# Attention's softmax jobs by twos, with bias and mask added on TensorE, in a two-block model on one NeuronCore

## The chip, the cores and the metric

One core of a Trainium2 chip runs the whole program. The metric is the device time of one execution in microseconds (us). The engines are named as the profile names them: PE (TensorE matmul; PEld is its weight load), DVE (VectorE), ACT (ScalarE), POOL (GpSimd), SP (SyncE, which issues DMAs). PE's results land in PSUM, which has 8 banks of 512 float32 per partition.

## What is computed

The program is a chain of two models of two layers each, over 512 positions of width 1024: first a mixer and a mixture-of-experts layer, twice, and then attention and a gated feed-forward layer, twice. Only the attention of the second model is touched. It has three kinds of heads, four of each, all computed by query blocks of 128:

```
def chunk_mask(qi, ki):
    return (ki[None, :] // CHUNK_2) <= (qi[:, None] // CHUNK_2)          # CHUNK_2 = 64
...
        sc = jnp.einsum('bhqd,bhkd->bhqk', qb, k).astype(jnp.float32) * scale
        p = jax.nn.softmax(sc + bias_fn(qi, ki), axis=-1).astype(v.dtype)
        return jnp.einsum('bhqk,bhkd->bhqd', p, v)
# fox:  bias = where(ki <= qi, cum[q] - cum[k], NEG), width 64, scale 64 ** -0.5
# diff: bias = where(chunk_mask, -slope[h] * abs(q - k), NEG), two softmaxes (q1 k1, q2 k2) of width 64 over one v of width 128
# mla:  bias = where(chunk_mask, 0, NEG), width 96, scale 96 ** -0.5, v of width 64
    x = x + jnp.concatenate([o_fox, o_diff, o_mla], axis=-1) @ w_o[i]
```

All is float32.

## The kernel before, in words

Each engine has its instruction list written out by hand; semaphores hand data over. `Handoff` is a kind of PSUM bank with a `full` and a `free` count; `Banks.take` goes round all 8 banks and makes PE wait until the last owner of a bank has freed it.

Attention of a layer is made of **jobs**: one head (or one of diff's two softmaxes) and one query block. Block qc sees n = 128 (qc + 1) keys, and the blocks go in the order 3, 1, 2, 0 (n = 512, 256, 384, 128). There are 16 mla jobs, 32 diff jobs and 16 fox jobs in each of the two layers. A job has three parts, and `pipeline` goes through them with a lag: at step m every engine does `turn` of job m - 3, `scores` of job m, `values` of job m - 4.

- `tensor_scores`: PE multiplies q (K rows by 128) with k (K rows by n) into a bank, as a plain float32 matmul, which the profile shows as two matmuls (two passes). K is 96 for mla and 64 for diff and fox: diff's two softmaxes lie on rows 0 to 63 and 64 to 127, and so do fox's even and odd heads. For fox two bf16 matmuls more add the bias (6 rows, L1915) and the causal mask of the last 128 columns (L1916).
- `vector_scores`: for mla and diff, DVE reads the bank, scales, adds the bias or mask (L2137, into SBUF tile PB) and takes the maximum (L2138). For fox it only takes the maximum from the bank (L2122). For each diff head DVE first makes that head's bias tile BT (L2128).
- `scalar_scores`: ACT takes the exponential with the row sum (L2029), from PB for mla and diff, from the bank for fox.
- `tensor_turn`, `scalar_turn`: PE transposes each 128 by 128 piece into a bank (L1931), and ACT copies it to SBUF (L2037).
- `tensor_values`, `vector_values`: PE multiplies with v (L1939), two passes for each 128 keys, and DVE scales by the reciprocal of the sum.

Between these parts lie products of the layer with its weights, on PE lines L600 and L602: v of diff (`dv`) after some diff steps, fox's q and k (`fqk`), fox's v (`fv`, 96 matmuls of 256 columns), and the output product, whose first half is followed by `rest_of_third`, the end of fox's jobs. During fox's steps 5 to 10 one transposed feature of the output (L508) is made at a step.

## Time and profile before

| | |
|---|---|
| time, median of 3 runs | 2738.56 us (2738.56 to 2741.27) |
| profiled execution, its own time | 2739.48 us |
| its span in the profile | 2738.1 us |
| PE busy | 2631.8 us (96%) |
| DVE, ACT, POOL busy | 1205.6, 909.4, 360.0 us |
| attention's jobs and products, layer 0 | about 1470 to 1670 us of the span |
| the same, layer 1 | about 2143 to 2345 us of the span |

In the rows below, a row of the timeline is one run of like instructions: its start, the time from its first start to its last end, engine, line, operation, tiles, shapes, count, and in brackets idle time before it. Matmuls overlap in their records (each has a latency), so what one costs is read from the distance between the starts of neighbouring rows. PEclk is the clock that TensorE was granted, 1.00 being full.

### The profile page before, as it was taken

To read this page: it belongs to the slowest core of one execution; us is meant where nothing else is said; L and a number is where in the kernel's file an instruction comes from. 1 tells how busy PE (TensorE), PEld (TensorE's weight loads), DVE (VectorE), ACT (ScalarE), POOL (GpSimd) and SP (SyncE) were. 2 spreads that over 40 slices of the span, in tenths; PEclk is the share of its full clock that TensorE was granted. 3 is DMA by queue.
4 is the path that set the end of the run, shared out by engine and by line. 5 is a ranking of instruction groups with operands and counts; after the bars stand their busy time and mean duration, and the time that the engine had idled before them with its cause. 6 is when DMAs were issued, how large, how long until landed. Compare 5 with 4: busy or idle time off the path is not lost.

```text
span 2738.1 us, 33170 instructions
## 1 busy us (share of the span) xinstructions
PE 2631.8 (96%) x13288; PEld 1828.3 (67%) x13288; DVE 1205.6 (44%) x2337; ACT 909.4 (33%) x1740; POOL 360.0 (13%) x167
## 2 busy tenths in 40 slices
PE   7989999999878999999989999999999999999999
PEld 6865444444756544445467678888888767888887
DVE  2543233232746223223357643562554664355264
ACT  4431111111473111111254453442345445443233
POOL 3200000000331000000020011222222101122122
PEclk9999999999998999999999999999999999999999
DMA  5229999999313999999822011223132101223212
GB/s 203 72 98 420 419 421 421 421 421 384 108 47 133 417 421 421 421 421 421 353 73 78 32 62 49 95 94 116 62 112 84 58 16 62 78 93 108 77 62 85
DMA packets 139004, 543.42 MB, mean 198 GB/s; under 512 B 18784, under 2 KB 30304, under 8 KB 89696
## 3 DMA queue, kind: packets, MB, share of 16 engines
q1 hardware_dynamic: 129232, 536.94, 50.2%
q10 hardware_dynamic: 9616, 4.32, 0.6%
q8 instruction: 108, 1.77, 0.3%
q14 instruction: 48, 0.39, 0.0%
HBM read 539.12 MB, written 2.10 MB: 198 GB/s over the span
## 4 chain that ended last, share of the span: by engine, by line
PE 93%; DVE 3%; ACT 2%; issue 1%; DMA 1%; POOL 0%; SPq 0%; DVEq 0%; ACTq 0%
PE ps L600 24%; PE ps L1362 16%; PE ps L602 15%; PE ps L1384 8%; PE ps L1337 5%; PE ps L622 4%; PE ps L534 3%; PE ps L1939 3%; PE ps L1397 3%; PE ps L1919 2%; PE ps L1398 2%; PE ps L1931 1%; PE ps L535 1%; PE ps L1914 1%; PE ps L452 1%
## 5 line engine op out<-in xcount | busy, mean ns | idle before, releaser
L600 PE MATMUL ps<-w,w 128*128 128x512 f32 x2976 | 681.5, 391 | 2.6 <-POOL w L277 2.6
L600 PEld LDWEIGHTS ps<-w,w 128*128 128x128 f32 x2976 | 560.3, 189 | 120.0 <-POOL w L277 3.4
L277 POOL TENSOR_TENSOR w<-w,w 128x1024 fp32r<-128x1024 f32 (+2 forms) x139 | 336.3, 2429 | 2219.0 <-ACT w L269 2219.0
L1362 PE MATMUL ps<-w,w 128*64 128x512 f32 x2048 | 451.6, 594 | 1.8 <-issue 1.8
L602 PE MATMUL ps<-w,w 128*128 128x512 f32 (+1 forms) x1872 | 416.4, 385 | 18.3 <-issue 15.2
L602 PEld LDWEIGHTS ps<-w,w 128*128 128x128 f32 x1872 | 345.0, 193 | 85.9 <-issue 19.8
L269 ACT ACTIVATE w<-w 128x1024 fp32r<-128x1024 f32 (+2 forms) x260 | 252.9, 1000 | 438.0 <-PE ps L600 197.4
L277 DVE TENSOR_TENSOR w<-w,w 128x1024 fp32r<-128x1024 f32 (+2 forms) x121 | 195.5, 1623 | 386.3 <-ACT w L269 383.9
L1362 PEld LDWEIGHTS ps<-w,w 128*64 128x64 f32 x2048 | 146.0, 137 | 285.6 <-issue 285.6
L1614 DVE TENSOR_TENSOR X<-ps,X 128x512 f32<-128x512 f32 x256 | 163.1, 683 | 163.2 <-PE ps L1398 162.2
L1384 PE MATMUL ps<-w,w 128*64 128x512 f32 x1024 | 226.8, 595 | 0.8 <-ACT w L1448 0.8
L2363 DVE SCALAR_TENSOR_TENSOR w<-ps,PK,w 128x511 f32<-128x511 f32 (+1 forms) x176 | 131.9, 749 | 75.5 <-ACT w L2319 72.4
L1384 PEld LDWEIGHTS ps<-w,w 128*64 128x64 f32 x1024 | 70.6, 137 | 139.8 <-issue 138.9
L1337 PE MATMUL ps<-w,w 128*128 128x256 f32 x1024 | 131.0, 287 | 4.9 <-DVE w L1585 4.9
L1337 PEld LDWEIGHTS ps<-w,w 128*128 128x128 f32 x1024 | 130.0, 196 | 7.6 <-DVE w L1585 5.1
L1602 DVE TENSOR_TENSOR w<-ps,w 128x512 f32<-128x512 f32 x32 | 34.8, 1086 | 212.0 <-PE ps L1362 212.0
L622 PE MATMUL ps<-w,w 128*128 128x512 f32 x528 | 122.0, 390 | 0.0
L1397 PE MATMUL ps<-w,w 128*128 128x512 f32 x256 | 111.8, 437 | 4.6 <-DVE w L1621 4.6
L1621 DVE SCALAR_TENSOR_TENSOR w<-ps,w,w 128x512 fp32r<-128x512 f32 x64 | 45.1, 747 | 159.0 <-ACT w L1493 159.0
L622 PEld LDWEIGHTS ps<-w,w 128*128 128x128 f32 x528 | 98.8, 188 | 20.3
L1493 ACT ACTIVATE w<-ps,w 128x512 fp32r<-128x512 f32 x64 | 40.6, 684 | 204.0 <-PE ps L1384 204.0
L534 PE MATMUL ps<-w,w 128*128 128x256 f32 x768 | 98.7, 292 | 9.7 <-POOL w L277 6.5
(256 smaller groups left out, 2471.0 us busy)
## 6 DMA issues: line engine op xcount, KB each, us to landing
w<-in_moe_w_gate SPq DMA_DIRECT2D x128, 1024.0 KB, 14.5
w<-in_moe_w_up SPq DMA_DIRECT2D x128, 1024.0 KB, 16.8
w<-in_moe_w_down SPq DMA_DIRECT2D x128, 1024.0 KB, 13.6
w<-in_w_up SPq DMA_DIRECT2D x40, 1024.0 KB, 5.1
w<-in_w_down SPq DMA_DIRECT2D x20, 1024.0 KB, 5.1
w<-in_w_in SPq DMA_DIRECT2D x16, 1024.0 KB, 5.1
w<-in_ab_w_in SPq DMA_DIRECT2D x10, 1024.0 KB, 5.2
w<-in_c_w_in SPq DMA_DIRECT2D x8, 1024.0 KB, 5.1
```

Of the source, the lines that this page charges most:

```text
L269: up(self.whi, self.S.e.activation(hi, raw, ACT.Copy))
L277: up(self.wlo[self.low[s][0]], lane.e.tensor_tensor(lo, raw, hi.bitcast(F32), ALU.subtract))
L534: return pe.matmul(bs[o][:, t], w[:, P * o:P * o + P], a(k)[:, t], start=first, stop=stop)
L600: ins = pe.matmul(bank[:, :], wp[:, k, P * o:P * o + P], ap(k0 + k), start=first, stop=stop)
L602: ins = pe.matmul(bank[:, 0:width], ap(k0 + k)[:, P * o:P * o + P], wp[:, k, :], start=first, stop=stop)
L622: ins = pe.matmul(bank_of(o)[:, 0:width], ap(k)[:, P * o:P * o + P], wp, start=(k == 0 and pi == 0), stop=(hi is rows[-1][0] and pi == 2))
L1337: i = pe.matmul(bank[:, 256 * k:256 * k + 256], HB[part][:, c, t:t + P], SELR[:, c, :], start=(part == 0 and c == 0), stop=(part == 1 and ...
L1362: ins = pe.matmul(bank[64 * e:64 * e + 64, :], XG[p % 3][:, 4 * u + k, 64 * e:64 * e + 64], w[e][:, k, :], start=(u == 0 and k == 0), stop ...
L1384: ins = pe.matmul(two[n][64 * e:64 * e + 64, :], HDT[:, 2 * u + k, 64 * e:64 * e + 64], w[e][:, k, 512 * n:512 * n + 512], start=(u == 0 a ...
L1397: pe.matmul(bank[:, :], s_, YH[:, 512 * n:512 * n + 512], start=True, stop=False)
L1614: up(bx.free, dve.tensor_tensor(x, bank[:, :], x, ALU.add))
L2363: ins = dve.scalar_tensor_tensor(y[:, d:T], bank[:, 0:T - d], col("conv_w_2", 132 * i + 44 * tap + f), y[:, d:T], ALU.mult, ALU.add)
```

## The change

Jobs are taken by twos. At step p each engine does `turn` of pair p - 2, `scores` of pair p, `values` of pair p - 3. A pair is two jobs of one list that follow each other: diff's two softmaxes of one head and block, fox's heads 0 and 1 (or 2 and 3) at one block, mla's blocks 3 and 1 (or 2 and 0) of one head. Both score matmuls of a pair are issued first, then the bias matmuls, then the masks: a far bias of diff for the columns ahead of the last 128 (3 rows, bf16), and for the last 128 columns a bf16 matmul of the identity with a constant tile that holds mask and near bias. The scales move into the copies of q. DVE's addition and its bias tiles are gone, ACT reads all scores from PSUM, and one reciprocal serves two jobs. Scores always take banks 0 to 3; everything else within attention's pipeline takes banks 4 to 7. The constants shrink from 1971 to 1715 words a row, and POOL's two casts at the start go.

```diff
-LAG = 3
 TAIL = 4
+ALL_BANKS, SCORE_BANKS, OTHER_BANKS = tuple(range(8)), (0, 1, 2, 3), (4, 5, 6, 7)
 BLOCKS = (3, 1, 2, 0)
...
+    ("identb", 64), ("causalb", 64), ("blockb", 64), ("nearb", 256), ("far_q", 256), ("far_k", 192),
...
-    def take(self, kind):
-        self.i = (self.i + 1) % 8
-        while self.t[self.i] in self.held:
-            self.i = (self.i + 1) % 8
-        if self.owner[self.i]:
-            before, k = self.owner[self.i]
+        self.PE, self.among, self.last = PE, ALL_BANKS, {ALL_BANKS: 7}
+    def take(self, kind, among=None):
+        among = among or self.among
+        i = self.last[among] = among[(among.index(self.last.get(among, among[-1])) + 1) % len(among)]
+        if self.owner[i]:
+            before, k = self.owner[i]
             self.PE.wait_total(before.free, k)
-        kind.banks.append(self.t[self.i])
-        self.owner[self.i] = (kind, len(kind.banks))
-        return self.t[self.i]
+        kind.banks.append(self.t[i])
+        self.owner[i] = (kind, len(kind.banks))
+        return self.t[i]
...
+                    for two in range(2) for qc in BLOCKS for h in (2 * two, 2 * two + 1)]
...
             scores, turn, values = engine
-            nj = len(jobs)
-            for m in steps:
-                if m in at_step:
-                    at_step[m]()
-                if LAG <= m < nj + LAG:
-                    turn(m0 + m - LAG, jobs[m - LAG])
-                if m < nj:
-                    scores(m0 + m, jobs[m])
-                if m > LAG:
-                    values(m0 + m - LAG - 1, jobs[m - LAG - 1])
+            for p in steps:
+                if p in at_step:
+                    at_step[p]()
+                for lag, part in ((2, turn), (0, scores), (3, values)):
+                    m = 2 * (p - lag)
+                    if 0 <= m < len(jobs):
+                        part(m0 + m, jobs[m:m + 2])
         def two_kinds(engine, dv, fqk):
-            n = len(mla_jobs) + len(diff_jobs)
-            pipeline(mla_jobs + diff_jobs, 0, engine, {M_DIFF + LAG: dv, n: fqk}, range(n + LAG + 1))
+            n = M_FOX // 2
+            pipeline(mla_jobs + diff_jobs, 0, engine, {M_DIFF // 2 + 2: dv, n: fqk}, range(n + 4))
         def third_kind(engine, fv, o_feature):
-            at_step = {LAG: fv}
-            for n, k in enumerate(FEATURES_OUT[:6]):
-                at_step[LAG + 2 + n] = lambda k=k: o_feature((k,))
-            pipeline(fox_jobs, M_FOX, engine, at_step, range(len(fox_jobs)))
+            at_step = {2: fv}
+            for n in range(3):
+                at_step[4 + n] = lambda n=n: o_feature(FEATURES_OUT[2 * n:2 * n + 2])
+            pipeline(fox_jobs, M_FOX, engine, at_step, range(len(fox_jobs) // 2))
...
-        def tensor_scores(m, job):
-            qc, kind, h, q, k, _, _ = job
-            n = P * (qc + 1)
-            if kind == "fox":
-                bank = banks.take(bfs)
-                of_head = slice(32 * h, 32 * h + 6)
+            n = len(fox_jobs) // 2
+            pipeline(fox_jobs, M_FOX, engine, {}, range(n, n + 4))
+        def tensor_scores(m, two):
+            taken = [banks.take(bsc, SCORE_BANKS) for _ in two]
+            for bank, (qc, _, _, q, k, _, _) in zip(taken, two):
+                n = P * (qc + 1)
                 pe.matmul(bank[:, 0:n], q, k[:, 0:n], start=True, stop=False)
-                pe.matmul(bank[:, 0:n], turned_q[of_head, P * qc:P * qc + P], turned_k[of_head, 0:n], start=False, stop=False)
-                up(bfs.full, pe.matmul(bank[:, n - P:n], CTB[:, 0, :], CTB[:, 1, :], start=False, stop=True))
-            else:
-                bank = banks.take(bsc)
-                up(bsc.full, pe.matmul(bank[:, 0:n], q, k[:, 0:n], start=True, stop=True))
-        def wait_exp(lane, m, job):
-            if job[1] == "fox":
-                lane.wait_ge(bfs.free, m - M_FOX + 1)
-            else:
-                lane.wait_ge(ex, m + 1)
-        def tensor_turn(m, job):
-            wait_exp(PE, m, job)
-            bank = banks.take(bpt)
-            for j in range(job[0] + 1):
-                ins = pe.transpose(bank[:, P * j:P * j + P], PB[m % (LAG + 1)][:, P * j:P * j + P], ident)
-            up(bpt.full, ins)
-        def tensor_values(m, job):
-            qc, vals, dv = job[0], job[5], job[6]
-            PE.wait_ge(bpt.free, m + 1)
-            bank = banks.take(bo)
-            for j in range(qc + 1):
-                ins = pe.matmul(bank[:, 0:dv], PTB[m % 2][:, P * j:P * j + P], vals(j), start=(j == 0), stop=(j == qc))
-            up(bo.full, ins)
+            for bank, (qc, kind, h, _, _, _, _) in zip(taken, two):
+                n = P * (qc + 1)
+                if kind == "fox":
+                    rows_ = slice(32 * h, 32 * h + 6)
+                    pe.matmul(bank[:, 0:n], turned_q[rows_, P * qc:P * qc + P], turned_k[rows_, 0:n], start=False, stop=False)
+                elif kind != "mla" and qc:
+                    rows_ = slice(64 * int(kind[-1]), 64 * int(kind[-1]) + 3)
+                    pe.matmul(bank[:, 0:n - P], far_q[rows_, P * h:P * h + P], far_k[rows_, T - n:T - P], start=False, stop=False)
+            for bank, (qc, kind, h, _, _, _, _) in zip(taken, two):
+                n = P * (qc + 1)
+                near = {"mla": cst_bf16("blockb"), "fox": cst_bf16("causalb")}.get(kind, near_diff[:, P * h:P * h + P])
+                up(bsc.full, pe.matmul(bank[:, n - P:n], cst_bf16("identb"), near, start=False, stop=True))
+        def tensor_turn(m, two):
+            for m, job in zip((m, m + 1), two):
+                PE.wait_ge(bsc.free, m + 1)
+                bank = banks.take(bpt)
+                for j in range(job[0] + 1):
+                    ins = pe.transpose(bank[:, P * j:P * j + P], PB[m % 4][:, P * j:P * j + P], ident)
+                up(bpt.full, ins)
+        def tensor_values(m, two):
+            for m, (qc, _, _, _, _, vals, dv) in zip((m, m + 1), two):
+                PE.wait_ge(bpt.free, m + 1)
+                bank = banks.take(bo)
+                for j in range(qc + 1):
+                    ins = pe.matmul(bank[:, 0:dv], PTB[m % 4][:, P * j:P * j + P], vals(j), start=(j == 0), stop=(j == qc))
+                up(bo.full, ins)
...
+            banks.among = OTHER_BANKS
             two_kinds(engine, values_of_diff, queries_of_fox)
...
-                    banks.held = bx.banks[-NT:]
+                    banks.among = OTHER_BANKS
                     rest_of_third(engine)
                     PE.wait_ge(bo.free, M_FOX + len(fox_jobs))
                     tensor_o_features(FEATURES_OUT[6:])
-                    banks.held = ()
+                    banks.among = ALL_BANKS
...
+            banks.among = SCORE_BANKS
...
-        def scalar_scores(m, job):
-            qc, kind, h = job[0], job[1], job[2]
-            n = P * (qc + 1)
-            p = PB[m % (LAG + 1)]
-            scores = p
-            if kind == "fox":
-                scores = bfs.next(S)
-                S.wait_ge(bpt.full, m - LAG)
-            S.wait_ge(mx, m + 1)
-            up(bfs.free if kind == "fox" else ex,
-               act.activation(p[:, 0:n], scores[:, 0:n], ACT.Exp, bias=AT[:, m % 8:m % 8 + 1],
-                              accum_out=AT[:, 8 + m % 8:9 + m % 8]))
-        def scalar_turn(m, job):
-            n = P * (job[0] + 1)
-            bank = bpt.next(S)
-            if m > 1:
-                S.wait_ge(bo.full, m - 1)
-            up(bpt.free, act.activation(PTB[m % 2][:, 0:n], bank[:, 0:n], ACT.Copy))
-        def scalar_values(m, job):
+        def scalar_scores(m, two):
+            for m, job in zip((m, m + 1), two):
+                n = P * (job[0] + 1)
+                bank = bsc.next(S)
+                if m > 3:
+                    S.wait_ge(bpt.full, m - 3)
+                S.wait_ge(mx, m + 1)
+                up(bsc.free, act.activation(PB[m % 4][:, 0:n], bank[:, 0:n], ACT.Exp, bias=AT[:, m % 8:m % 8 + 1],
+                                            accum_out=AT[:, 8 + m % 8:9 + m % 8]))
+        def scalar_turn(m, two):
+            for m, job in zip((m, m + 1), two):
+                n = P * (job[0] + 1)
+                bank = bpt.next(S)
+                if m > 3:
+                    S.wait_ge(bo.full, m - 3)
+                up(bpt.free, act.activation(PTB[m % 4][:, 0:n], bank[:, 0:n], ACT.Copy))
...
-            scalar_product(("dq", i), scalar_banks(lambda m: DQ[:, m, :]))
+            scalar_product(("dq", i), scalar_banks(lambda m: DQ[:, m, :], scale=0.125))
...
-                    bank_to(T_[0:96, h, :], bank[0:96, :])
+                    bank_to(T_[0:96, h, :], bank[0:96, :], scale=96 ** -0.5 if T_ is QT else 1.0)
...
-        def vector_scores(m, job):
-            qc, kind, h = job[0], job[1], job[2]
-            n = P * (qc + 1)
-            if kind == "fox":
-                bank = bfs.next(V)
+        def vector_scores(m, two):
+            for m, job in zip((m, m + 1), two):
+                n = P * (job[0] + 1)
+                bank = bsc.next(V)
                 up(mx, dve.tensor_reduce(AT[:, m % 8:m % 8 + 1], bank[:, 0:n], AX, ALU.max, negate=True))
-                return
-            scale = 96 ** -0.5 if kind == "mla" else 0.125
-            if kind == "diff0" and qc == BLOCKS[0]:
-                if h > 1:
-                    V.wait_ge(bsc.free, m - 8)
-                vstep(dve.scalar_tensor_tensor(BT[:, h % 2, :], cst("dist"), -slopes[h], mask, ALU.mult, ALU.add))
-            if kind == "mla":
-                bias = mask[:, 512 - n:512]
-            else:
-                bias = BT[:, h % 2, 512 - n:512]
-            p = PB[m % (LAG + 1)][:, 0:n]
-            bank = bsc.next(V)
-            if m > LAG:
-                V.wait_ge(bpt.full, m - LAG)
-            V.wait_total(bsc.free, up(bsc.free, dve.scalar_tensor_tensor(p, bank[:, 0:n], scale, bias, ALU.mult, ALU.add)))
-            up(mx, dve.tensor_reduce(AT[:, m % 8:m % 8 + 1], p, AX, ALU.max, negate=True))
-        def vector_turn(m, job):
-            wait_exp(V, m, job)
-            sm = AT[:, 8 + m % 8:9 + m % 8]
+        def vector_turn(m, two):
+            V.wait_ge(bsc.free, m + 2)
+            sm = AT[:, 8 + m % 8:10 + m % 8]
             up(rc, dve.reciprocal(sm, sm))
...
-                    up(bv.free, dve.tensor_copy(T_[0:96, h, :], bank[0:96, :]))
+                    up(bv.free, dve.tensor_scalar(T_[0:96, h, :], bank[0:96, :], 96 ** -0.5 if T_ is QT else 1.0, None, ALU.mult))
...
-            up(ctb, pool.tensor_copy(CTB[:, j, :], cst(name)))
```

PE's instruction order in diff's jobs, layer 0, before: the end of a step, two jobs of block 3 (128x512 scores of w_20480 and w_22528, which are DQ and DK; w_16384 is v, w_14336 the copied transposes). `order` counts a float32 matmul once.

```order
L1931 MATMUL ps<-CT,w_12288_11029 128x128 [waits s_scores_free,s_exp]
L1931 MATMUL ps<-CT,w_12288_11029 128x128 x2
L1919 MATMUL ps<-w_22528_11038,w_20480_11036 128x512 [waits s_values_free]
L1939 MATMUL ps<-w_16384_11039,w_14336_11030 128x128 [waits s_turned_free]
L1939 MATMUL ps<-w_16384_11039,w_14336_11030 128x128 x2
L1931 MATMUL ps<-CT,w_12288_11029 128x128 [waits s_scores_free,s_exp]
L1919 MATMUL ps<-w_22528_11038,w_20480_11036 128x512 [waits s_values_free]
L1939 MATMUL ps<-w_16384_11039,w_14336_11030 128x128 [waits s_turned_free]
L1939 MATMUL ps<-w_16384_11039,w_14336_11030 128x128 x2
```

The same place now (L1912 scores, L1920 far bias, L1924 near bias and mask):

```order
L1931 MATMUL ps<-CT,w_12288_11027 128x128 [waits s_turned_free,s_scores_free]
L1931 MATMUL ps<-CT,w_12288_11027 128x128 x2
L1931 MATMUL ps<-CT,w_12288_11027 128x128 [waits s_turned_free,s_scores_free]
L1931 MATMUL ps<-CT,w_12288_11027 128x128 x2
L1912 MATMUL ps<-w_22528_11035,w_20480_11033 128x512 x2
L1920 MATMUL ps<-CT 128x384 x2
L1924 MATMUL ps<-CT 128x128 x2
L1939 MATMUL ps<-w_16384_11036,w_14336_11028 128x128 [waits s_values_free]
L1939 MATMUL ps<-w_16384_11036,w_14336_11028 128x128
L1939 MATMUL ps<-w_16384_11036,w_14336_11028 128x128 [waits s_values_free]
L1939 MATMUL ps<-w_16384_11036,w_14336_11028 128x128
```

The two score matmuls now stand next to each other, with two transposes' groups before them and two values' groups behind, and each turn waits for the copy (s_turned_free) of the pair before, in the same two banks.

PE's order in fox's jobs, layer 0, before (junk holds the bias's parts, CTB the identity and the mask):

```order
L1931 MATMUL ps<-CT,w_12288_11029 128x128 [waits s_values_free]
L1931 MATMUL ps<-CT,w_12288_11029 128x128
L1914 MATMUL ps<-w_20480_11042 128x512 [waits s_bank_feat_free]
L1915 MATMUL ps<-junk 128x512
L1916 MATMUL ps<-CTB 128x128
L1939 MATMUL ps<-w_22528_11043,w_14336_11030 128x64 [waits s_turned_free]
L1939 MATMUL ps<-w_22528_11043,w_14336_11030 128x64 x3
```

And a fox step now:

```order
L1931 MATMUL ps<-CT,w_12288_11027 128x128 [waits s_values_free,s_scores_free] x2
L1912 MATMUL ps<-w_20480_11039 128x256 x2
L1917 MATMUL ps<-junk 128x256 x2
L1924 MATMUL ps<-CT 128x128 x2
L1939 MATMUL ps<-w_22528_11040,w_14336_11028 128x64 [waits s_bank_feat_free]
L1939 MATMUL ps<-w_22528_11040,w_14336_11028 128x64 x2
L1939 MATMUL ps<-w_22528_11040,w_14336_11028 128x64 [waits s_bank_feat_free]
L1939 MATMUL ps<-w_22528_11040,w_14336_11028 128x64 x2
```

The same three forms of matmul are there for each job, now in twos of each form; the values' banks are now freed by the features (s_bank_feat_free) made in the same step.

## Rows read from the trace of the kernel before

**Rows 1.** The page: PE's busy time; the chain that ended last, by engine.

```profile
PE 2631.8 (96%) x13288; PEld 1828.3 (67%) x13288; DVE 1205.6 (44%) x2337; ACT 909.4 (33%) x1740; POOL 360.0 (13%) x167
...
PE 93%; DVE 3%; ACT 2%; issue 1%; DMA 1%; POOL 0%; SPq 0%; DVEq 0%; ACTq 0%
```

**Rows 2.** Windows: stretch, length, busy PE, PEld, DVE, ACT, POOL, PEclk, DMA.

```profile
1476.58:1493.30 16.72, 16.72 (x114) 13.12 (x114) 14.89 (x49) 11.64 (x39) 0.00 (x0) 1.00 0.01 1
1529.50:1571.40 41.90, 41.90 (x228) 27.44 (x227) 35.20 (x111) 23.31 (x72) 0.00 (x0) 1.00 0.00 1
1615.00:1642.00 27.00, 27.00 (x169) 17.66 (x166) 13.69 (x43) 15.23 (x44) 2.42 (x1) 1.00 0.25 79
```

**Rows 3.** Timeline of PE, diff's jobs, layer 0.

```profile
1529.58 1.12 PE L1919 MATMUL ps<-w,w 64*128 64x512 f32 x2
...
1542.27 0.48 PE L1919 MATMUL ps<-w,w 64*128 64x128 f32 x2
1542.69 0.71 PE L1939 MATMUL ps<-w,w 128*128 128x128 f32 x4
1543.23 0.49 PE L1931 MATMUL ps<-CT,w 128*128 128x128 f32 x3
1543.65 1.12 PE L1919 MATMUL ps<-w,w 64*128 64x512 f32 x2
1544.71 0.94 PE L1939 MATMUL ps<-w,w 128*128 128x128 f32 x6
```

**Rows 4.** Timeline of PE, the bf16 transposes ahead of mla's jobs, and mla's jobs, layer 0.

```profile
1469.81 0.61 PE L1983 MATMUL ps<-CTB,w 128*128 128x128 bf16 x8
...
1481.13 1.02 PE L1919 MATMUL ps<-w,w 96*128 96x512 f32 x2
1482.07 1.10 PE L1939 MATMUL ps<-w,w 128*128 128x64 f32 x8
...
1486.65 1.02 PE L1919 MATMUL ps<-w,w 96*128 96x512 f32 x2
```

**Rows 5.** Timeline of PE, fox's jobs, layer 0.

```profile
1632.79 0.60 PE L1931 MATMUL ps<-CT,w 128*128 128x128 f32 x4
...
1634.50 1.12 PE L1914 MATMUL ps<-w 64*128 64x512 f32 x2
1635.56 0.39 PE L1915 MATMUL ps<-junk 6*128 6x512 bf16 x1
1635.88 0.23 PE L1916 MATMUL ps<-CTB 128*128 128x128 bf16 x1
1635.94 1.06 PE L1939 MATMUL ps<-w,w 128*128 128x64 f32 x8
...
1640.66 0.61 PE L1931 MATMUL ps<-CT,w 128*128 128x128 f32 x4
```

**Rows 6.** The chain, experts' matmuls on column halves (64 of 128 columns).

```profile
218.60 13.97 PE ps L1362 x64
```

**Rows 7.** Timeline of PE: first turn of mla, values behind fqk.

```profile
1474.37 0.66 PE L1931 MATMUL ps<-CT,w 128*128 128x128 f32 x4 [1.35 <-ACT w L2029]
...
1595.36 0.94 PE L1939 MATMUL ps<-w,w 128*128 128x128 f32 x6 [0.91 <-ACT w L2037]
```

**Rows 8.** Windows: the fv product of layer 0 and of layer 1.

```profile
1600.87:1614.11 13.24, 13.24 (x98) 13.03 (x97) 9.37 (x23) 11.37 (x34) 2.59 (x1) 0.87 0.06 25
...
2274.79:2288.99 14.20, 14.20 (x98) 13.99 (x97) 10.86 (x24) 10.96 (x31) 2.52 (x1) 0.80 0.04 15
```

**Rows 9.** Lines by form, fox's jobs: count, busy us, mean ns.

```profile
L2037 ACT ACTIVATE w<-ps 128x512 f32<-128x512 f32 x4 | 2.4, 590 | 0.0
...
L2029 ACT ACTIVATE w<-ps,AT 128x512 f32<-128x512 f32 x3 | 2.1, 688 | 4.3 <-DVE AT L2122 4.3
L2122 DVE TENSOR_REDUCE AT<-ps 128x1 f32<-128x512 f32 x3 | 2.1, 684 | 2.8 <-PE ps L1916 2.8
```

**Rows 10.** The chain, its first piece.

```profile
2.74 13.75 DMA w<-in_ab_w_in
```

More of the change, by code:

```diff
@@ L1852, in attention @@
         turned_q, turned_k = junk[:, 0:T], junk[:, T:2 * T]
-        mask = cst("mask")
+        near_diff, far_q, far_k = (cst_bf16(name) for name in ("nearb", "far_q", "far_k"))
         lam_init = 0.8 - 0.6 * math.exp(-0.3 * i)
-        slopes = [2.0 ** (-2.0 * (h + 1)) for h in range(4)]
         up_unit = W.of[("up", i)][0]
@@ new lines, in vector_turn, with vector_values @@
+        def vector_turn(m, two):
+            V.wait_ge(bsc.free, m + 2)
+            sm = AT[:, 8 + m % 8:10 + m % 8]
+            up(rc, dve.reciprocal(sm, sm))
+        def vector_values(m, two):
+            for m, (qc, kind, h, _, _, _, dv) in zip((m, m + 1), two):
+                sm = AT[:, 8 + m % 8:9 + m % 8]
+                bank = bo.next(V)
+                V.wait_ge(rc, m // 2 + 1)
+                if kind == "diff0":
+                    up(bo.free, dve.tensor_scalar(O1B[:, qc, :], bank[:, 0:dv], sm, None, ALU.mult))
+                elif kind == "diff1":
+                    V.wait_ge(nlam, 1)
+                    V.wait_ge(bo.free, m)
+                    vstep(dve.tensor_tensor(sm, sm, LS[:, 3:4], ALU.mult))
+                    o = O[:, qc, 256 + P * h:384 + P * h]
+                    up(bo.free, dve.scalar_tensor_tensor(o, bank[:, 0:dv], sm, O1B[:, qc, :], ALU.mult, ALU.add))
+                else:
+                    c0 = (768 if kind == "mla" else 0) + 64 * h
+                    up(bo.free, dve.tensor_scalar(O[:, qc, c0:c0 + 64], bank[:, 0:dv], sm, None, ALU.mult))
```

74 lines of the change are left out of this document (31 added, 43 removed).

## The prediction

> **What bounds it now.** I read the page first: PE is busy 2631.8 of 2738.1 us and 93% of the chain is PE [rows 1]. So only PE time, or a wait of PE, is worth anything. Then the windows of the three kinds of jobs: PE is busy through all of 16.72, 41.90 and 27.00 us, while DVE has 14.89, 35.20 and 13.69 and ACT 11.64, 23.31 and 15.23 [rows 2]. The addition that DVE loses is therefore cover, not path; what counts is PE's instruction list, and whether the others still keep ahead of it.
>
> Then the timeline, by distances between starts. A score matmul of a 64-row job takes 0.42 us for 128 columns and 1.06 for 512 [rows 3]. The difference, 0.64, is three times 128 columns in two passes: **0.107 us for a pass of 128 columns**. A head has 4 + 2 + 3 + 1 = 10 such pieces. An mla head (96 rows) takes 1486.65 - 1481.13 = 5.52 [rows 4]: less 20 pieces in passes (2.13) that leaves 3.39 for 10 transposes and 20 passes of values, **0.113 each**, and nothing over. A diff head has 8 jobs in 1543.65 - 1529.58 = 14.07 [rows 3]: 60 x 0.113 = 6.78 and 40 x 0.107 = 4.27 leave 3.02, so **0.38 us a job is lost to the 64-row form**. It shows where PE changes form: 0.42 - 0.21 = 0.21 in the scores, 0.42 - 3 x 0.11 = 0.09 between transposes and scores, 0.54 - 4 x 0.113 = 0.09 at the first values. I split it into entering the form (0.20: drain and a weight load that shows) and leaving it (0.20). A fox head takes 1640.66 - 1632.79 = 7.87 [rows 5]: 3.39 + 2.13, bias 0.53 (512 columns in 0.32, of which 0.11 is a change of form, so 0.053 for 128), four masks of 0.06, and 1.58 over, 0.39 a job.
>
> The Trainium skill (TensorEngine Tiling, Key Properties) says that changing the tiling mode drains TensorE; the trace agrees, with 0.38 for a 64-row job and none for a 96-row one.
>
> **The change, part by part.** (1) *Diff.* A pair enters the 64-row form once (0.20), leaves through the 3-row form and back (0.20), not twice each. Its passes are issued A1 A2 B1 B2. A1 and A2 share rows and follow each other, B2 follows B1; only A2 and B1 can run at once, so I count three passes for four. That two tiles of the array do run at once is shown only for column halves: 64 matmuls of 512 columns in 13.97 us are 0.218 each [rows 6], half of a pass of 512 (0.427). I carry that over to row halves, with 0.04 for the late start of the second (between nothing and a weight load, 0.11). Far bias, bf16 on rows 0 and 64: 0.053 for 128 columns, also side by side, + 0.04. Two near masks 0.12. A head then has 3 x 10 x 0.107 = 3.20, far bias 6 x 0.053 = 0.32, three pairs with fixed 0.20 + 0.04 + 0.20 + 0.04 + 0.12 = 0.60, and one without far bias 0.46, so 2.26, and 6.78 as before: 12.56 against 14.07, -1.5; eight heads **-12.0**.
>
> (2) *Fox*, two heads: 3.20 + 0.53 + 4 x 0.60 + 6.78 = 12.91 against 2 x 7.87 = 15.74, -2.8; four such twos **-11.3**.
>
> (3) *Mla* gets a mask matmul for each job and no overlap (96 rows). The eight bf16 transposes take 0.61 [rows 4], about 0.06 each in a stream; 32 x 0.06 = **+1.9** (bounds 0 and 0.113 each: 0 to +3.6).
>
> (4) *Waits.* At mla's start PE waits 1.35 us for the first exponential [rows 7], after three jobs' scores. Now four jobs' scores go first (2.5 us of work), and the first exponential needs scores of 1.45, a maximum of 0.69 and an exponential of 0.69 [rows 9] with some 0.4 of handing over: 3.3, a wait of about 0.8. With the smaller wait for the first copy gone: -0.7 a layer, **-1.4**. Behind fqk the values wait 0.91 for ACT's copy [rows 7], since ACT first empties four banks and splits a weight; a longer list (pair's turn and another pair's values) covers part: -0.4 a layer, **-0.8**. Bounds for both: 0 and -5.
>
> (5) *Nothing:* DVE's addition, the bias tiles, half of the reciprocals, exponentials from PSUM (688 ns for 512, fox already does it [rows 9]): all beside PE. If DVE's cover were gone, it would have shown in mla, where DVE is at 14.89 of 16.72. *Constants:* 256 words less on 128 rows is 0.13 MB ahead of the first weights, whose landing begins the chain [rows 10]: **-0.3**. *Banks:* scores' four are asked for again two steps on, when their exponentials are needed anyway. Turned and values now have two banks each. The tight chain is ACT's: after a block 3 pair's scores come a maximum of 0.69, two exponentials of 0.79 with their sums, two copies of block 1 or 2 (0.4 to 0.5) and handovers, 3.3 to 3.5 us, before the next turn but one may take its banks; PE has 0.9 of values and a step of 2.9 to do meanwhile. It fits by 0.3 to 0.5. Products take the same four banks one each 0.7 us, so the last values are emptied in time. 0, bounds 0 and +6.
>
> Sum: -12.0 - 11.3 + 1.9 - 1.4 - 0.8 - 0.3 = **-23.9**. From 2739.5, the profiled execution's own time, that is 2715.6; the median of the runs is 0.9 lower, so **2715 us**.
>
> By the Trainium skill (TensorE: Matmul & The Clock Gate, Part 3) four row tiles gave 3.07 times, not 4; an estimate from that is 1.3 passes for two at once, 0.3 x 10 x 0.107 x 12 = +4, and 2719. No row here shows row tiles.
>
> **Rivals.** *No overlap on rows.* Nothing in this trace shows two row halves at once. Then a diff head has 4.27 + 0.64 + 2.0 + 6.78 = 13.7 (-0.4, eight: -3), and fox's two heads 4.27 + 1.07 + 2.1 + 6.78 = 14.2 (-1.5, four: -6): only the changes of form are saved. With the rest (-0.6), **2729**.
>
> *Overlap, but each second tile shows its weight load*, since B's weights come only when A2 has begun: + 0.11 for 48 pairs, +5: **2720**. For it: the first matmul after a change of form shows its load. Against: the column halves show none [rows 6].
>
> *Slower: the banks in two pools.* If ACT's chain above is longer than PE's 3.8 us, every turn waits. It decides from 24 / 64 pairs = 0.37 us a pair, so from a chain of about 4.2. A chain of 4.4 costs 0.6 a pair, 38 us: 2715 + 38 = **2753**. Against: DVE has nothing left in the chain but the maximum.
>
> *The clock.* In the fv products it is 0.87 and 0.80 of full [rows 8], so 13.24 and 14.20 us would be 11.5 and 11.4 at 2.4 GHz: 4.5 us lost behind fox's first, scores-only steps. I leave that as it is. If it goes, 2710; if it doubles, 2720. If all of diff fell to 1.2 GHz, its passes (3.20 a head) would double: 8 x 3.2 = +26 at least, 2741. Against: diff's 41.90 us are at 1.00 today [rows 2], with as many transposes and values.
>
> The Trainium skill (the same page, Part 4) says that transposes don't count as busy for the clock; in diff's stretch a fifth of the work is transposes, and the clock is full.
>
> **The numbers.** Chances: three passes for four 0.58, shown weight loads 0.14, no overlap 0.17, banks 0.04, clock low in a whole stage 0.03, something else 0.04. The likeliest alone: 2709 to 2721 (mask 0 to 0.113, waits 0 to -5, clock -4.5 to +4.5). The range takes in no overlap: **2707 to 2730**. Within 0.2% (5.5 us, about what a measurement of this kernel can tell from no change) is 2733 to 2744. Faster: 0.58 + 0.14 + 0.17 = 0.89; same 0.04; slower 0.07.
>
> **What would show it.** A diff head of 12.6 us and two fox heads of 12.9 in PE's timeline; A2 and B1 starting within 0.04 us; an mla head of 5.8; no idle time ahead of the turns in mid-stage; a first wait of 0.8; fv as now. It is wrong if B1 starts a pass later than A2, or if turns wait for L2037's successor on ACT.

## The result, and the profile after

| | before | after |
|---|---|---|
| time, median of the runs | 2739.12 us (2738.56 to 2741.27) | 2703.57 us (2702.28 to 2704.16) |
| profiled execution, its own time | 2739.48 us | 2703.67 us |
| span | 2738.1 us | 2702.3 us |

The ratio is 0.9868, 95% interval 0.9851 to 0.9885: faster by 1.3%, or 35.8 us between the profiled executions. Predicted were 23.9 us less and at least 2707, so the gain is larger than the range allowed.

The page after; first PE's busy time, then the chain that ended last by engine. PE is the bound as before [rows 1], and DVE's share of the chain has grown from 3 to 5%:

```profile
PE 2592.2 (96%) x13432; PEld 1818.3 (67%) x13432; DVE 1148.7 (43%) x2169; ACT 899.4 (33%) x1740; POOL 360.3 (13%) x165
...
PE 90%; DVE 5%; ACT 2%; issue 2%; DMA 0%; POOL 0%; SPq 0%; DVEq 0%; ACTq 0%
```

PE's timeline of a diff head after (L1912 scores, L1920 far bias, L1924 near bias, L1939 values, L1931 transposes), the answer to [rows 3]:

```profile
1528.07 1.13 PE L1912 MATMUL ps<-w,w 64*128 64x512 f32 x4
1529.13 0.34 PE L1920 MATMUL ps<-CT 3*128 3x384 bf16 x2
1529.40 0.29 PE L1924 MATMUL ps<-CT 128*128 128x128 bf16 x2
1529.53 1.11 PE L1939 MATMUL ps<-w,w 128*128 128x128 f32 x8
...
1536.28 0.49 PE L1912 MATMUL ps<-w,w 64*128 64x128 f32 x4
...
1539.41 1.13 PE L1912 MATMUL ps<-w,w 64*128 64x512 f32 x4
```

Here is the miss. Four matmuls of 512 columns (two jobs, two passes each) take 1.06 us from the first start to the next row's, the distance that before held two [rows 3]. The trace has their single starts: 1528.073 and 1528.080 us for the first pass of each job, 1528.606 and 1528.613 for the second. Both passes of the second job cost nothing. A head is 1539.41 - 1528.07 = 11.34 us against 14.07.

The windows of the stages: before, from the first mla score to the dv product (once), from the end of dv to fqk (once), and from the end of fqk to the second half of the output product (both layers); columns as in [rows 2].

```profile
1470.84:1497.78 26.94, 25.33 (x157) 18.35 (x157) 22.56 (x68) 18.20 (x52) 0.00 (x0) 1.00 0.13 41
1519.42:1571.30 51.88, 51.19 (x281) 33.75 (x280) 41.04 (x130) 29.41 (x88) 1.27 (x1) 1.00 0.07 22
1592.95:1658.90 65.95, 62.84 (x383) 47.86 (x382) 31.56 (x88) 36.51 (x107) 7.35 (x3) 0.97 0.15 49
2266.35:2333.78 67.43, 64.32 (x384) 48.83 (x382) 31.56 (x88) 36.68 (x107) 7.22 (x3) 0.95 0.15 48
```

The same after:

```profile
1471.75:1498.56 26.81, 24.90 (x176) 19.42 (x177) 12.82 (x41) 18.25 (x57) 0.00 (x0) 1.00 0.12 41
1520.23:1561.25 41.02, 40.33 (x322) 30.47 (x321) 23.01 (x80) 26.75 (x87) 1.27 (x1) 1.00 0.08 27
1582.90:1642.32 59.42, 54.12 (x394) 44.96 (x393) 32.12 (x82) 35.49 (x108) 8.00 (x3) 1.00 0.17 54
2235.80:2296.86 61.06, 55.76 (x394) 45.72 (x393) 32.23 (x82) 35.71 (x108) 8.01 (x3) 0.97 0.16 53
```

Mla gives nothing (-0.13 a layer), diff 10.86 a layer, fox with its products 6.53 and 6.37: 34.9 us. In fox's stage PE sits idle more, 59.42 - 54.12 = 5.3 us for 3.1 before, and in mla's 1.9 for 1.6: 5.0 us in both layers. These are the longest new waits, in PE's timeline (the first turn of mla; the first feature of the output in fox). The values behind that feature wait 0.39 us, and the turn behind the fv product 0.92 us where it waited 0.47 before:

```profile
1476.34 0.89 PE L1931 MATMUL ps<-CT,w 128*128 128x128 f32 x6 [1.91 <-ACT w L2027]
...
1610.31 1.07 PE L511 MATMUL ps<-CT,w 128*128 128x128 f32 x8 [1.85 <-ACT w L2036]
```

### The profile page after: what moved, and what is told of

It reads as the page before. It is cut to its first block, busy times and chain, and to the rows that moved or that the text cites. A ratio compares the mean times of both kernels' runs of the same rounds, so it can differ in the third digit from the quotient of the medians.

```text
span 2702.3 us, 33251 instructions
## 1 busy us (share of the span) xinstructions
PE 2592.2 (96%) x13432; PEld 1818.3 (67%) x13432; DVE 1148.7 (43%) x2169; ACT 899.4 (33%) x1740; POOL 360.3 (13%) x165
## 4 chain that ended last, share of the span: by engine, by line
PE 90%; DVE 5%; ACT 2%; issue 2%; DMA 0%; POOL 0%; SPq 0%; DVEq 0%; ACTq 0%
PE ps L603 23%; PE ps L1363 16%; PE ps L605 14%; PE ps L1385 8%; PE ps L1338 5%; PE ps L625 4%; PE ps L537 4%; PE ps L1398 3%; PE ps L1939 2%; PE ps L1399 2%; PE ps L1912 2%; PE ps L1931 1%; PE ps L538 1%; PE ps L455 1%; DVE w L278 1%
## 5 line engine op out<-in xcount | busy, mean ns | idle before, releaser
L605 PE MATMUL ps<-w,w 128*128 128x512 f32 (+1 forms) x1872 | 410.9, 381 | 18.2 <-issue 15.2
```

What stands on the lines that cost most here:

```text
L605: ins = pe.matmul(bank[:, 0:width], ap(k0 + k)[:, P * o:P * o + P], wp[:, k, :], start=first, stop=stop)
```

## The experiments

All start from the changed kernel and are timed against the kernel before (2736.5 to 2741.1 us in these runs). The order is that of the questions: the overlap, DVE, the banks, the waits.

**e1_apart**, nothing side by side:

```diff
-            for bank, (qc, _, _, q, k, _, _) in zip(taken, two):
+            for bank, (qc, kind, h, q, k, _, _) in zip(taken, two):
                 n = P * (qc + 1)
                 pe.matmul(bank[:, 0:n], q, k[:, 0:n], start=True, stop=False)
-            for bank, (qc, kind, h, _, _, _, _) in zip(taken, two):
-                n = P * (qc + 1)
                 if kind == "fox":
...
-            for bank, (qc, kind, h, _, _, _, _) in zip(taken, two):
-                n = P * (qc + 1)
                 near = {"mla": cst_bf16("blockb"), "fox": cst_bf16("causalb")}.get(kind, near_diff[:, P * h:P * h + P])
```

> The changed kernel with one thing put back: of a pair of jobs, all products of the first (scores, far or Fox bias, near bias) are issued, and then all of the second, so nothing of a pair stands side by side and the row form is entered and left twice a pair. Theory: both row halves run both fp32 passes at once, so a diff head (11.34 us after the change) loses 10 blocks x 2 passes x 0.107 = 2.14 us of overlap, up to 0.32 us of overlap of the far products, and 4 pairs x 0.39 us of form changes = 1.56 us: about 15.3 us, and two fox heads gain 2.14 + 0.5 + 1.56 = 4.2 us; all in all 8 x 4.0 + 4 x 4.2 = +49 us, 2752 us. Rival (what I predicted, three passes for four): 10 x 0.107 = 1.07 us less in each, 8 x 2.95 + 4 x 3.1 = +36 us, 2740 us. Rival (the gain came from banks, exponentials from PSUM and the clock): less than +15 us.

Measured: 2750.71 us (2749.69 to 2751.45), ratio 1.004 (1.0025 to 1.0055). That is +47 on the changed kernel, and 11 us slower than before: everything else in the change together costs that much. PE's timeline, one diff head:

```profile
1531.83 1.12 PE L1912 MATMUL ps<-w,w 64*128 64x512 f32 x2
1532.89 0.33 PE L1918 MATMUL ps<-CT 3*128 3x384 bf16 x1
...
1533.31 1.12 PE L1912 MATMUL ps<-w,w 64*128 64x512 f32 x2
...
1547.12 1.12 PE L1912 MATMUL ps<-w,w 64*128 64x512 f32 x2
```

15.29 us a head, as the theory had it (15.3). Before the change a head took 14.07; the 1.22 us more, with the bias matmuls that PE now has, are 9.8 of these 11 us in eight heads.

**e2_same_rows**, overlap and form changes apart:

```diff
-                     for h in range(4) for qc in BLOCKS for s in range(2)]
+                     for h in range(4) for s in range(2) for qc in BLOCKS]
-                    for two in range(2) for qc in BLOCKS for h in (2 * two, 2 * two + 1)]
+                    for h in range(4) for qc in BLOCKS]
```

> The changed kernel with the jobs in another order: both jobs of a pair are on the same row half (two blocks of one diff half, two blocks of one fox head), so the row form is still entered and left only once a pair, and nothing can run side by side. Theory (two passes run in the time of one, form changes apart): diff head 11.34 + 2.14 + up to 0.32 = 13.5 to 13.8 us, two fox heads +2.1 to +2.7 us, together 8 x 2.3 + 4 x 2.4 = +28 us (26 to 31), 2729 to 2735 us. Rival, three passes for four: diff head 12.4 to 12.7, together +13 to +17 us, 2718 us. Rival, the fewer form changes are the gain and the overlap is worth nothing: 0, 2704 us.

Measured: 2729.03 us (2728.59 to 2734.24), ratio 0.9962 (0.9946 to 0.9977): +25.5. PE's timeline; the pair is 512 and 256 columns on one row half, then 512 columns of the next head:

```profile
1530.40 1.55 PE L1912 MATMUL ps<-w,w 64*128 64x512 f32 x4
...
1544.28 1.55 PE L1912 MATMUL ps<-w,w 64*128 64x512 f32 x4
```

A head is 13.88 us: 2.54 more than side by side, of which 20 passes of 0.107 are 2.14; the other 0.40, the far bias matmuls among them, were not taken apart. Overlap is worth 2.54 us a head, the saved form changes 15.29 - 13.88 = 1.41. Two passes in the time of one is shown; three passes for four (a head of 12.4 to 12.7) is out.

**e3_unequal**, do the halves wait for each other? In `fox_jobs` the odd head takes block {3: 1, 1: 3, 2: 0, 0: 2}[qc].

> The changed kernel with fox pairs of unequal blocks on the two row halves: 512 columns with 256, 256 with 512, 384 with 128, 128 with 384. Theory A (each row half has its own queue and never waits for the other): of the pair of 512 and 256 the short job's second pass starts when its first is done, 0.27 us after it, while the long job's first pass still runs to 0.53 us; the pair takes 8 x 0.107 = 0.86 us plus what is left, as long as the long one alone, about 1.06 us. Theory B (one order for both, the second passes start together after both first passes): the two second passes start within 0.02 us of each other at 0.53 us. Either way a pair costs what its longer job costs: 4 + 4 + 3 + 3 blocks for 4 + 2 + 3 + 1, 4 x 2 x 0.107 = 0.86 us more for two fox heads, +3.4 us, 2707 us. Theory C (they run one after another when unequal): +8 to +10 us.

Measured in one run: 2707.31 us. The starts of the four matmuls of the pair of 512 and 256 columns, from the trace (start us, distance to the one before, duration ns):

```
1612.387          693  64x512
1612.394  0.007   480  64x256
1612.714  0.320   376  64x256
1612.921  0.207   589  64x512
```

The short job's second pass starts 0.32 us behind its first and 0.21 us before the long job's second: theory A. Each row half goes through its own matmuls. The Trainium skill (TensorE: Matmul & The Clock Gate, Part 3) says that matmuls start and end in program order. The first passes do, 7 ns apart, but here the second pass of the job issued last starts 0.207 us ahead of the other job's second pass, so for the passes of two tiles the measurement decides. The time, a single run, can't tell the theories A and B apart; the starts do.

**e4_dve_back** and **e9_dve_one_pool**, VectorE's pass put back (its result is overwritten, so only its time counts; unlike before the change, the maximum and the exponential still read PSUM), with two pools and with one ring (the edit of e5):

```diff
                 bank = bsc.next(V)
+                if m < M_FOX:
+                    if m > 3:
+                        V.wait_ge(bpt.full, m - 3)
+                    vstep(dve.tensor_scalar(PB[m % 4][:, 0:n], bank[:, 0:n], 1.0, None, ALU.mult))
```

> The changed kernel with a pass of VectorE over the scores put back in each job of Mla and Diff: it copies the bank of scores to the tile of probabilities (which the exponential then overwrites) before the maximum is taken, as much work as the addition of bias and mask in the kernel before. Theory: VectorE, busy 35.20 us of 41.90 us in the diff heads before (11.7 us a head), stands above the 11.34 us that TensorE now needs, so it becomes the bound and the diff head goes to 11.8 to 12.4 us: 8 x 0.5 to 8 x 1.0 = +4 to +8 us, 2708 to 2712 us. Rival (my prediction: the addition lies beside TensorE, its removal is worth nothing): within 1 us, 2704 us.

> The changed kernel with VectorE's pass over the scores put back (as in e4, 2726.0 us) and the banks in one ring of eight (as in e5, 2699.8 us). In e4 a diff head went from 11.34 to 13.55 us though VectorE was busy only 31.18 of 40 us: TensorE's value products waited for a bank that VectorE empties, up to 0.93 us twice a head. Theory: the cost in e4 is the short pool (the values of one step need the banks of the values of the step before, which VectorE empties only behind its passes over the newest scores); with one ring these banks are older, and the diff head falls to 11.4 to 12.2 us: 2702 to 2712 us. Rival: VectorE's own work is the bound whatever the banks: diff head above 13 us, 2720 us or more.

Measured: e4 2726.01 us (2725.7 to 2728.66), ratio 0.9956 (0.9942 to 0.9969), +22.4; e9 2716.49 us (2715.55 to 2718.6), ratio 0.9918 (0.9905 to 0.9932), +16.7 on e5. Windows of one diff head, e4, with the longer of PE's two waits in it (the other is 0.86 us):

```profile
1530.81:1544.36 13.55, 11.77 (x92) 8.63 (x91) 10.64 (x33) 7.72 (x25) 0.00 (x0) 1.00 0.01 2
...
1541.72 2.05 PE L1939 MATMUL ps<-w,w 128*128 128x128 f32 x16 [0.93 <-DVE w L2137]
```

and e9, with two rows of its ACT timeline and one of its two waits of PE (the other is 0.39 us):

```profile
1528.31:1541.40 13.09, 12.19 (x91) 8.78 (x90) 10.29 (x32) 7.46 (x25) 0.00 (x0) 1.00 0.01 2
...
1537.88 0.58 ACT L2027 ACTIVATE w<-ps,AT 128x384 f32<-128x384 f32 x1 [1.05 <-DVE AT L2124]
...
1539.51 0.65 ACT L2036 ACTIVATE w<-ps 128x256 f32<-128x256 f32 x2
...
1538.60 2.21 PE L1939 MATMUL ps<-w,w 128*128 128x128 f32 x16 [0.37 <-ACT w L2027]
```

Both expectations for e4 (2708 to 2712, and 2704) are far off in size, and e9 lies between its two (2702 to 2712, and 2720 or more). DVE has 10.3 to 10.6 us of work in a head, less than PE's 11.34, and yet the head takes 13.1 to 13.6: so the sum of its work doesn't bind. I read the rows as a chain of three engines in order: ACT's copies of turned probabilities stand behind exponentials that wait for maxima (1.05 us here) that stand behind the extra pass, and PE waits for ACT. What each link costs was not tried by itself. The pools' part is 0.46 us a head; the rest stays with one ring. So the dropped addition is no bonus beside the overlap but, in this order of work, a condition of it: with DVE's pass a head gains 0.5 us with two pools (14.07 to 13.55) and 1.0 with one ring, of the 2.7 without it.

**e5_one_pool**:

```diff
-            taken = [banks.take(bsc, SCORE_BANKS) for _ in two]
+            taken = [banks.take(bsc) for _ in two]
...
-            banks.among = OTHER_BANKS
+            banks.among = ALL_BANKS
             two_kinds(engine, values_of_diff, queries_of_fox)
```

> The changed kernel with the banks in one ring of eight, as before the change, in place of four for scores and four for the rest, in all three kinds of attention; a pair of fox steps also needs a bank or two for the features. Theory: two pools cost TensorE a wait of 1.85 us in each layer (features wait for a turned bank); with one ring the features take banks that came free long ago or those of scores whose exponentials are late, so this wait changes by no more than 2 us a layer, and nothing changes in mla and diff: 2700 to 2705 us. Rival: the two pools are what lets scores run ahead, and one ring makes them wait for the exponentials in every step, 0.1 us or more in each of 96 steps: 2713 us or more.

Measured: 2699.84 us (2699.11 to 2700.05), ratio 0.9855 (0.984 to 0.987): 3.7 us less than the changed kernel. Windows of e5, diff's stage and fox's in both layers:

```profile
1519.04:1560.07 41.03, 40.34 (x323) 30.48 (x321) 23.05 (x80) 26.76 (x87) 1.27 (x1) 1.00 0.08 27
1581.71:1639.96 58.25, 53.90 (x394) 44.87 (x393) 32.16 (x82) 35.18 (x108) 8.00 (x3) 1.00 0.17 55
2233.51:2293.06 59.55, 55.27 (x394) 46.20 (x393) 32.35 (x82) 35.37 (x108) 8.01 (x3) 0.97 0.17 54
```

Diff is the same to 0.01 us; fox gains 1.2 and 1.5 us, most of it since the features' wait falls to 1.0 us. The pools bring nothing here. The remaining 1.2 us of the profiled executions lie ahead of diff's stage, where e5 has the same instructions: the first mla score comes at 1470.56 us for 1471.75. In the profiled executions of the changed kernel and all its variants it lies between 1469.5 and 1472.6 us, so a microsecond or two of a whole time says nothing about an edit.

**e6_features_later** (`at_step[5 + n]` for `at_step[4 + n]`) and **e7_table_early**:

```diff
             bank_to(junk[:, :], bank[:, :].bitcast(BF16))
+            S.wait_total(one, one.n)
+            up(one, act.activation(ONE[:, 1:2], ONE[:, 0:1], ACT.Exp))
```

> The changed kernel with the features of the output taken one step later in the fox stage (pair steps 5, 6 and 7 for 4, 5 and 6). Theory: the wait of 1.85 us in each layer stands there since the features need a bank whose copy comes behind exponentials and maxima that VectorE takes late; a step later the copies are done, the transposes of the next step find their exponentials ready, and 1.0 to 1.85 us a layer come back, and about 1 us of granted clock in the second layer: -2 to -5 us, 2699 to 2701.5 us. Rival: the lateness is VectorE's backlog of 6.68 us of low parts and norms, and the transposes wait there in place of the features: within 1 us, 2703.5 us.

> The changed kernel with a small exponential on ScalarE right behind the last copy before the first scores, so that the table load of 1.28 us, which in the changed kernel stands between the first maximum and the first exponential, lies in ScalarE's idle time of 1.83 us. Theory: TensorE's first wait goes from 1.91 to about 0.7 us (I had predicted 0.8), in both layers: -2.4 us, 2701.2 us; the wait before the change was 1.35 us. Rival: the first transposes wait for something else too (weights, a bank), less than 0.5 us a layer: 2703 us.

Measured: e6 2705.76 us (2704.78 to 2709.79), ratio 0.9883 (0.9868 to 0.9898); e7 2707.25 us (2701.98 to 2709.11), ratio 0.988 (0.9865 to 0.9895). Neither is faster; e7, expected at 2701.2, came to 2702 in one run and to 2706 to 2709 in three. In e6 the wait only moved, to the transposes, as the rival had it (PE's timeline):

```profile
1609.94 0.85 PE L1931 MATMUL ps<-CT,w 128*128 128x128 f32 x6 [1.84 <-ACT w L2036]
```

In e7 the wait went as wanted. ScalarE's timeline in the changed kernel, the table load on the path:

```profile
1474.21 1.28 ACT L2027 ACT_TABLE_LOAD   x1 [1.83 <-DVE AT L2120]
1475.51 0.69 ACT L2027 ACTIVATE w<-ps,AT 128x512 f32<-128x512 f32 x1
```

and in e7, with PE's first turn (1.91 us of wait before):

```profile
1471.04 1.28 ACT L2086 ACT_TABLE_LOAD   x1
...
1472.87 0.69 ACT L2027 ACTIVATE w<-ps,AT 128x512 f32<-128x512 f32 x1 [0.33 <-DVE AT L2122]
...
1473.70 0.89 PE L1931 MATMUL ps<-CT,w 128*128 128x128 f32 x6 [0.64 <-ACT w L2027]
```

The time went to the clock. Windows of e7: fox's jobs of layer 0, second half of the output product (layer 0), a product of 96 matmuls, fox's jobs of layer 1:

```profile
1599.17:1623.96 24.79, 21.66 (x164) 16.70 (x162) 17.28 (x35) 16.04 (x48) 4.83 (x2) 0.93 0.27 85
1641.17:1653.54 12.37, 12.37 (x48) 10.08 (x48) 3.30 (x5) 1.56 (x2) 2.37 (x1) 0.86 0.27 85
2098.49:2121.74 23.25, 23.25 (x98) 19.06 (x97) 20.86 (x130) 4.64 (x6) 2.40 (x1) 0.93 0.42 154
2255.27:2282.20 26.93, 24.16 (x163) 18.48 (x162) 17.46 (x35) 16.28 (x48) 4.82 (x2) 0.81 0.24 79
```

and the same four in the changed kernel:

```profile
1601.81:1625.10 23.29, 20.14 (x163) 15.36 (x162) 17.18 (x35) 15.58 (x48) 4.83 (x2) 1.00 0.28 91
1642.32:1653.07 10.75, 10.75 (x48) 8.90 (x48) 3.30 (x5) 1.56 (x2) 2.39 (x1) 1.00 0.30 98
2098.02:2119.67 21.65, 21.65 (x98) 17.92 (x98) 19.26 (x128) 4.64 (x6) 2.41 (x1) 1.00 0.45 165
2254.71:2279.65 24.94, 21.78 (x164) 16.12 (x162) 17.29 (x35) 15.80 (x48) 4.84 (x2) 0.93 0.25 85
```

1.50 + 1.62 + 1.60 + 1.99 = 6.7 us lost at the same instructions, more than the 2.6 gained; the first mla score came 1.4 us earlier, and that makes up the 2.6 us between the two profiled executions. The product of 96 matmuls takes 23.3 us in some of the kernels here, the one before among them, and 21.65 in others. Why the clock fell in these places, and whether taking the wait away has to do with it, isn't shown; the same edit on e5 gains 2.9 us (e11 below).

**e10 to e13**, for a better version: one ring and the early table (e11), both with later features (e10), one ring with DVE's two low parts behind the third step's maxima (e12), and e12 with the early table (e13). The last edit, without the lines of one ring:

```diff
-        def third_kind(engine, fv, o_feature):
+        def third_kind(engine, fv, o_feature, later=None):
...
+            if later:
+                at_step[3] = later
...
             def norm_and_low():
                 norm_of_diff()
-                vector_product(("fv", i))
...
-            third_kind(engine, norm_and_low, vector_o_features)
+            third_kind(engine, norm_and_low, vector_o_features, lambda: vector_product(("fv", i)))
```

> The changed kernel with one ring of eight banks (e5, 2699.8 us), the small exponential ahead of the first scores (e7) and the features a step later (e6). Theory: e7 takes 1.28 us off TensorE's first wait in each layer whatever the banks, and what it did not bring in time (2707.3 us instead of 2701.2) was lost to stretches of a granted clock of 0.86 to 0.93, each 1.6 us long in products that take 10.77 or 21.65 us otherwise; with one ring the features' wait is 1.0 us and a step later the transposes of the next step stand in their place: -2.6 us from the first wait, 0 to -1 from the features, and 0, 1 or 2 stretches of low clock more or less: 2694 to 2701 us. Rival: the waits taken away are given back by the clock again: 2699 to 2703 us.

> As e10 without the later features: one ring of eight banks and the small exponential. Theory: 2699.8 - 2.6 = 2697.2 us, and one stretch of low clock (1.6 us) more or less: 2695 to 2699 us. Rival: the clock gives the wait back as in e7, 2699 to 2703 us.

> The changed kernel with one ring of eight banks, and VectorE's two low parts of 3.3 us each, which stand ahead of the maxima of the third fox step, put behind them. Theory: these 6.68 us are what makes maxima, exponentials and copies late and so the features' wait (1.0 us with one ring, 1.85 us with two pools); behind the maxima the wait goes in both layers and no product waits for the low parts: -2 us, and less of a low clock in the second layer's fox stage: 2696 to 2698.5 us. Rival: the low parts are needed 6.68 us later by the output product or by the maxima of the fourth step, and the wait moves there: 2699 to 2701 us.

> As e12 with the small exponential of e7 as well: one ring, the table load early, the low parts behind the maxima. Theory: the gains add, 2699.8 - 2.6 - 2 = 2695 us (2693 to 2698). Rival: the clock gives back what the waits bring: 2698 us or more.

| | us | ratio to before (95%) |
|---|---|---|
| e10_ring_later_table | 2702.6 (2701.46 to 2705.74) | 0.9863 (0.9848 to 0.9878) |
| e11_ring_table | 2696.96 (2696.86 to 2697.99) | 0.9845 (0.9831 to 0.9858) |
| e12_ring_lows | 2697.19 (2696.91 to 2697.64) | 0.9845 (0.9831 to 0.9858) |
| e13_all | 2695.89 (2695.03 to 2696.33) | 0.9839 (0.9825 to 0.9852) |

e13 beats both kernels, the changed one by 7.7 us. e11 and e12 came out as expected, 2.9 and 2.7 us below e5. e13 is within its range, 0.9 above its 2695 and 4.0 below e5, less than both gains together. Its profiled execution lost time where nothing was edited: the first mla score came at 1471.37 us (e5 1470.56). Counted from that score to the end, e11, e12 and e13 are 2.1, 2.3 and 4.5 us shorter than e5, so there the gains add. e10, expected at 2694 to 2701, is where its rival had it, and its runs lie 4 us apart. In its profiled execution, the slowest of the four, fox's jobs ran at a clock of 0.87 in both layers. Its PE timeline shows the low level where the transposes of the next step waited:

```profile
1608.35 1.45 PE L1931 MATMUL ps<-CT,w 128*128 128x128 f32 x6 [0.92 <-ACT w L2027]
1609.73 2.08 PE L1912 MATMUL ps<-w 64*128 64x512 f32 x4
```

A pair of 512 takes 2.01 us instead of 1.06, that is 1.2 GHz instead of 2.4.

In e12 the wait for the features (1.0 us in e5) is gone, though not quite for the reason that I gave. VectorE's low parts in the changed kernel, and GpSimd's beside them:

```profile
1601.36 6.68 DVE L278 TENSOR_TENSOR w<-w,w 128x1024 fp32r<-128x1024 f32 x2
...
1601.00 2.67 POOL L278 TENSOR_TENSOR w<-w,w 128x1024 fp32r<-128x1024 f32 x1 [13.69 <-ACT w L270]
1603.98 2.98 POOL L278 TENSOR_TENSOR w<-w,w 128x1024 fp32r<-128x1024 f32 x1 [0.31 <-ACT w L270]
```

and in e13:

```profile
1604.40 2.35 DVE L278 TENSOR_TENSOR w<-w,w 128x1024 fp32r<-128x1024 f32 x2
...
1602.03 2.35 POOL L278 TENSOR_TENSOR w<-w,w 128x1024 fp32r<-128x1024 f32 x1 [0.32 <-ACT w L270]
```

Beside GpSimd's the two take 6.68 us, alone 2.35. Before the change they took 2.35 in layer 0, where GpSimd was idle but for the last 0.2 us. In layer 1 the first of them already met GpSimd's instruction and the second did not:

```profile
2284.41 2.52 POOL L277 TENSOR_TENSOR w<-w,w 128x1024 fp32r<-128x1024 f32 x1 [13.66 <-ACT w L269]
2284.59 3.43 DVE L277 TENSOR_TENSOR w<-w,w 128x1024 fp32r<-128x1024 f32 x1
2287.94 1.21 DVE L277 TENSOR_TENSOR w<-w,w 128x1024 fp32r<-128x1024 f32 x1
```

Each of VectorE's slow ones ends 1.1 us after the end of the GpSimd instruction beside it (1604.75 and 1603.67, 1608.03 and 1606.96, 2288.02 and 2286.93 us), which is nearly all of its 1.2 us alone: beside GpSimd's it hardly gets on at all. The Trainium skill (GPSIMD Engine Reference, Specifications) says that the two engines contend for SBUF when VectorE reads two SBUF inputs; the traces agree, at 3.4 us for 1.2.

After the change each of VectorE's two meets one of GpSimd's, in both layers. The scores of fox's third step were ready at about 1605.4 us and VectorE took their maxima at 1608.03, 2.6 us late, and the wait of 1.85 us stands behind these. With 2.35 us for the low parts VectorE would have been free at 1603.7, in time even in the old order; that is an estimate from these rows and wasn't tried.

## Why the prediction was right or wrong

- **The step that failed is "I count three passes for four", from "only A2 and B1 can run at once".** I let B1 wait for A2 since it is issued behind it. The row halves don't wait for each other: A1 and B1 start 7 ns apart, and so do A2 and B2 (the changed kernel's starts above; the overlap is worth 2.54 us a head by e2). Two passes for four had no chance of its own. The row that I leaned on could have told me: the first four matmuls of [rows 6], two column halves by turns, start at 218.603, 218.610, 219.054 and 219.090 us, so there too both first passes start together; with only A2 and B1 at once the first start would stand alone. Two passes for four take another 10 x 0.107 = 1.07 us off each diff head and each two fox heads, 12 x 1.07 = 12.8 us: -23.9 becomes -36.7, against -35.8 between the profiled executions. That this is so near is in part luck: the waits came out 7.2 us worse than the -2.2 that I had for them, and the clock about 5.5 us better than left as it was. The sizes around it held: 12.56 - 1.07 = 11.49 a diff head, measured 11.34; the pass of 0.107 and the form changes of 0.39 a job (1.41 for four pairs, counted 1.56).
- **Waits: predicted -1.4 and -0.8.** The first turn of mla waited 1.91, not 0.8 (1.35 before), as ScalarE now loads the exponential's table behind the wait for scores and not before it: 1.28 us that I had not listed. Behind fqk 0.56 against 0.91, -0.7 in two layers, as predicted. Fox's first feature waits 1.85 us that I had at nothing, and the values behind it and the turn behind fv wait 0.4 us more each. PE's idle time in the windows of mla and fox grew by 5.0 us in both layers.
- **"Nothing: DVE's addition": wrong as an argument, right as a sum.** Its removal is no term of its own only as long as the heads are long. A pass like it put back costs 22.4 us; by [rows 2] DVE had 35.20 us in three heads, 11.7 a head, and that already stood above the head of 11.34.
- **Mla's masks +1.9.** A head is now 5.73 against 5.52, +0.21 (eight heads +1.7): right.

```profile
1481.90 1.46 PE L1912 MATMUL ps<-w,w 96*128 96x512 f32 x4
...
1487.63 0.59 PE L1912 MATMUL ps<-w,w 96*128 96x512 f32 x1
```

- **Banks 0 (0 to +6).** Two pools cost fox about 2.7 us in both layers together (e5), nothing in diff. The rival *banks in two pools*, 2753, is out.
- **The clock, left as it was.** The fv products [rows 8] run at 1.00 now and take 1.49 and 2.44 us less (12.96 to 11.47, 13.92 to 11.48 between first and last start). Two further products of before at 0.86 and 0.93 are at 1.00 after, 1.6 us each. These 7 us about pay for the 5.0 us of waits, a low clock of 1.6 in layer 1's fox stage, and 0.9 us by which the first mla score comes later. That 0.9 is within the scatter told of under e5, and so are the constants' -0.3.

Of the rivals, *no overlap on rows* gave 2729, and e2, which is just that, measured 2729.03. Its diff head of 13.7 was near the 13.88 measured; that the whole is right to 0.1 us is luck, since waits and clock were off there as above. *Shown weight loads* is out: the second job starts 7 ns behind the first, not 0.11 us. So is the 2719 of 1.3 passes for two at once: two take the time of one.

## What to carry to other kernels

Two float32 products of 64 rows each, one on each half of the rows and issued one behind the other, cost what the longer of them costs (1.06 us for 512 columns with 512 or with 256); look for such pairs first. Read next what each of the other engines needs for one unit of work and in what order: an engine below the new bound can still set the pace through its place in a chain, and work that two engines share (here the low parts) can slide on top of each other. And a microsecond of wait taken away can be hidden by stretches of lower clock elsewhere, as in e7, so a small edit has to be judged by the windows of several products, not by its own wait or by the whole time alone.
